# A read of PSUM ahead of the maxima, and spread factors copied by VectorE: two transformer layers on one core

## The reference

```python
for l in range(DEPTH):                      # DEPTH = 2
    h = rms_norm(x, attn_norm[l])
    proj = h @ w_in[l]
    q_lat, kv_lat, k_rope, nsa_q, nsa_kv, gate_logits = jnp.split(proj, SPLIT_POINTS, axis=-1)
    o_mla = mla_attention(...)              # 8 heads: softmax(q k^T) v, causal
    o_nsa = nsa_attention(...)              # per head: g0*o_cmp + g1*o_slc + g2*o_win
    x = x + jnp.concatenate([o_mla, o_nsa], axis=-1) @ w_out[l]
    h = rms_norm(x, ffn_norm[l])
    x = x + conv_ffn(h, ffn_w_up[l], ffn_conv_w[l], ffn_conv_b[l], ffn_w_down[l])
return rms_norm(x, final_norm)
```

## Time and profile before

| | |
|---|---|
| median of 3 runs | 1331.05 us |
| profiled execution, time | 1330.93 us |
| profiled execution, span of the core | 1329.1 us |
| granted TensorE clock, mean | 0.997 of full speed |
| TensorE busy | 1272.4 us, 96% |
| VectorE busy | 693.0 us, 52% |
| ScalarE busy | 658.0 us, 50% |
| attention steps, first layer | about 118 to 262 us |
| attention steps, second layer | about 769 to 913 us |

### The profile page before, as it was taken

The page is one execution under the profiler, slowest core; times in us unless marked ns, Lnnn a source line. Parts: engine busy times, 40 slices in busy tenths (PEclk is TensorE's granted clock), DMA queues, the critical chain, the costliest instruction groups (busy, mean ns, idle before and its releaser), DMA issues.

```text
span 1329.1 us, 18517 instructions
## 1 busy us (share of the span) xinstructions
PE 1272.4 (96%) x6626; PEld 1052.8 (79%) x6626; DVE 693.0 (52%) x1196; ACT 658.0 (50%) x1225; POOL 66.1 (5%) x153
## 2 busy tenths in 40 slices
PE   5999988999999999999999999889999999999997
PEld 4997666788888888888889867667788888888886
DVE  6435666545555555533363456673645555554334
ACT  4336788634545454323252478793444545443323
POOL 1004110001000000000000211100000000000000
PEclk9999999999999999999999999999999999999999
DMA  6320100124333333322133210012233333333211
GB/s 218 104 90 17 65 1 30 52 64 124 95 95 95 95 95 95 125 98 95 53 90 101 73 64 1 1 49 65 77 97 95 95 95 95 95 95 127 95 63 64
DMA packets 121624, 107.56 MB, mean 81 GB/s; under 512 B 3890, under 2 KB 110996, under 8 KB 121568
## 3 DMA queue, kind: packets, MB, share of 16 engines
q1 hardware_dynamic: 119344, 102.71, 25.3%
q0 software_dynamic: 1360, 3.45, 0.9%
q10 hardware_dynamic: 864, 0.66, 0.2%
HBM read 104.71 MB, written 2.10 MB: 80 GB/s over the span
## 4 chain that ended last, share of the span: by engine, by line
PE 87%; DVE 6%; ACT 3%; issue 1%; DMA 1%; SPq 0%; DVEq 0%
PE ps L1411 24%; PE ps L1412 24%; PE ps L1413 24%; PE ps L1638 4%; PE ps L1591 4%; PE ps L1572 2%; DMA raw<-in_w_in_dram 1%; PE ps L1578 1%; PE ps L1577 1%; DVE probs L1163 1%; DVE probs L1044 1%; ACT probs L842 1%; DVE x L1064 1%; DVE w_lo L575 1%; PE ps L1650 1%
## 5 line engine op out<-in xcount | busy, mean ns | idle before, releaser
L1411 PE MATMUL ps<-ht_hi,w_hi 128*128 128x512 f32 (+2 forms) x776 | 297.9, 384 | 2.5 <-DVE w_lo L575 2.5
L1412 PE MATMUL ps<-ht_lo,w_hi 128*128 128x512 f32 (+2 forms) x776 | 296.6, 382 | 0.0
L1413 PE MATMUL ps<-ht_hi,w_lo 128*128 128x512 f32 (+2 forms) x776 | 296.4, 382 | 0.0
L575 DVE TENSOR_TENSOR w_lo<-raw,w_hi 128x1024 fp32r<-128x1024 f32 (+4 forms) x196 | 218.7, 1140 | 102.3 <-ACT w_hi L568 92.7
L568 ACT ACTIVATE w_hi<-raw 128x1024 fp32r<-128x1024 f32 (+4 forms) x196 | 187.2, 982 | 100.7 <-PE ps L1413 97.1
L1327 DVE SCALAR_TENSOR_TENSOR conv<-ps,cols,conv 128x510 f32<-128x510 f32 (+1 forms) x176 | 127.6, 746 | 181.4 <-ACT conv L963 175.6
L1411 PEld LDWEIGHTS ps<-ht_hi,w_hi 128*128 128x128 f32 x776 | 146.3, 189 | 31.2 <-DVE w_lo L575 2.9
L1412 PEld LDWEIGHTS ps<-ht_lo,w_hi 128*128 128x128 f32 x776 | 146.4, 189 | 27.9 <-issue 0.5
L1413 PEld LDWEIGHTS ps<-ht_hi,w_lo 128*128 128x128 f32 x776 | 146.4, 189 | 27.7
L1411 PE MATMUL ps<-w_hi,ht_hi 128*128 128x430 f32 (+1 forms) x392 | 148.3, 378 | 4.7 <-DVE ht_lo L1051 4.0
L963 ACT ACTIVATE conv<-ps,cols 128x512 f32<-128x512 f32 x88 | 68.1, 774 | 159.9 <-PE ps L1413 159.7
(11 more groups left out here) (185 smaller groups left out, 1531.3 us busy)
## 6 DMA issues: line engine op xcount, KB each, us to landing
raw<-in_ffn_w_up_dram SPq DMA_DIRECT2D x88, 512.0 KB, 4.3
raw<-in_ffn_w_down_dram SPq DMA_DIRECT2D x44, 512.0 KB, 3.3
raw<-in_w_in_dram SPq DMA_DIRECT2D x32, 430.0 KB, 3.5
raw<-in_w_out_dram SPq DMA_DIRECT2D x16, 512.0 KB, 4.0
raw<-in_nsa_cmp_w_dram SPq DMA_DIRECT2D x8, 512.0 KB, 3.7
x<-in_x_dram SPq DMA_DIRECT2D x4, 512.0 KB, 6.2
raw<-in_mla_w_uq_dram SPq DMA_DIRECT2D x4, 384.0 KB, 3.0
out_dram<-x SPq DMA_DIRECT2D x3, 512.0 KB, 2.6
```

Of the source, the lines that this page charges most:

```text
L575: last = nc.vector.tensor_tensor(d(w_lo)[:, :, d0:d1], r(raw)[:, :, r0:r1], d(w_hi)[:, :, d0:d1].bitcast(F32), ALU.subtract)
L1411: mm(o, lhs[0], rhs[0], start=start, stop=False)
L1412: mm(o, lhs[0], rhs[1], start=False, stop=False)
L1413: return mm(o, lhs[1], rhs[0], start=False, stop=stop)
```

## The change

Three things change.

1. The addition of the compressed output to the even group's result leaves `normalize` and becomes `add_compressed(r)`, with a semaphore of its own, `cmp_read`. VectorE runs it at step 4g+8 of the odd group g, ahead of the maxima of that step. `values` of groups 6, 8 and 10 waits for `cmp_read` in place of `sum_done`.
2. ScalarE's `evac_factors` goes. VectorE copies the spread factors itself, in `normalize`, right ahead of the multiplication, and increments `fac_out` there.
3. `spread(g)` moves on TensorE from step 4g+6 to step 4g+7, ahead of `compressed` and `values`. The two tables of bank uses follow it, and the transposes get bank 5 two steps later than before.

```diff
 SCORE_USES = [(use, (0, 1, 2)) for s in range(U + LAG)
               for use in (turn_uses(s) if s < U else []) +
-              ([("f", (s - T_LAG) // T)] if s >= T_LAG and (s - T_LAG) % T == T - 1 and s < U else [])]
-TURN_USES = [(use, (3, 4) if s <= PC_STEP[1] else (3, 4, 5) if s < U else (4, 5)) for s in range(T_LAG, U + LAG)
+              ([("f", (s - LAG) // T)] if s >= LAG and (s - LAG) % T == T - 1 and s < U else [])]
+TURN_USES = [(use, (3, 4) if s <= PC_STEP[1] + 2 else (3, 4, 5) if s < U else (4, 5)) for s in range(T_LAG, U + LAG)
              for use in (turn_uses(s - T_LAG) if s < U + T_LAG else []) +
-             ([("f", NG - 1)] if s == U + T_LAG - 1 else [])]
+             ([("f", NG - 1)] if s == U + LAG - 1 else [])]
...
-                def evac_factors(g):
-
-                    act.wait_ge(fac_done, at(fac_done, l, g + 1))
-                    activate(onorm[:, g % 2, :], ps[:, FAC_BANK[g][0], :], ACT.Copy).then_inc(fac_out, 1)
...
-                    if LAG <= s < U + LAG and (s - LAG) % T == T - 1:
-                        evac_factors((s - LAG) // T)
...
+                def add_compressed(r):
+
+                    dve.wait_ge(cmp_done, at(cmp_done, l, r + 1))
+                    tt(onorm[:, 0, :], ps[:, 6, :], onorm[:, 0, :], ALU.add).then_inc(cmp_read, 1)
+
                 def normalize(g):
 
                     f = onorm[:, g % 2, :]
-                    if g >= H // 2 and g % 2 == 1:
-                        dve.wait_ge(cmp_done, at(cmp_done, l, (g - H // 2) // 2 + 1))
-                        f0 = onorm[:, 0, :]
-                        tt(f0, ps[:, 6, :], f0, ALU.add).then_inc(dve_chain, 1)
+                    dve.wait_ge(fac_done, at(fac_done, l, g + 1))
+                    v.tensor_copy(f, ps[:, FAC_BANK[g][0], :]).then_inc(fac_out, 1)
+                    dve.wait_ge(fac_out, at(fac_out, l, g + 1))
                     dve.wait_ge(pv_done, at(pv_done, l, 2 * g + 2))
-                    dve.wait_ge(fac_out, at(fac_out, l, g + 1))
                     tt(f, ps[:, out_bank(g), :], f, ALU.mult).then_inc(on_done, 1)
                     if g >= H // 2 and g % 2 == 1:
-                        dve.wait_ge(dve_chain, ch.next())
+                        dve.wait_ge(cmp_read, at(cmp_read, l, (g - H // 2) // 2 + 1))
                         dve.wait_ge(on_done, at(on_done, l, g + 1))
-                        tt(f, f, f0, ALU.add).then_inc(sum_done, 1)
+                        tt(f, f, onorm[:, 0, :], ALU.add).then_inc(sum_done, 1)
...
+                    if s > LAG + U_MLA and (s - LAG - 1 - U_MLA) % (2 * T) == 2 * T - 1:
+                        add_compressed((s - LAG - 1 - U_MLA) // (2 * T))
                     if s < U:
                         row_max(s)
...
                     elif g > H // 2 and g % 2 == 0:
-                        pe.wait_ge(sum_done, at(sum_done, l, (g - H // 2) // 2))
+                        pe.wait_ge(cmp_read, at(cmp_read, l, (g - H // 2) // 2))
...
+                    if s >= LAG and (s - LAG) % T == T - 1:
+                        spread((s - LAG) // T)
                     if s >= LAG + U_MLA and (s - LAG - U_MLA) % (2 * T) == 2 * T - 1:
                         compressed((s - LAG - U_MLA) // (2 * T))
                     if s >= LAG and s % 2 == 1:
                         values(s - LAG)
-                    if T_LAG <= s < U + T_LAG and (s - T_LAG) % T == T - 1:
-                        spread((s - T_LAG) // T)
```

More of the change, by code:

```diff
@@ L157 @@
     "sc_done": 2 * U, "max_done": 2 * U, "exp_done": 2 * U, "t_done": 6 * NG, "pt_act": U, "pt_second": U // 2,
-    "fac_ready": NG, "fac_done": NG, "fac_out": NG, "on_done": NG, "cmp_done": H // 2, "sum_done": H // 2, "pv_done": U // 2,
+    "fac_ready": NG, "fac_done": NG, "fac_out": NG, "on_done": NG, "cmp_done": H // 2, "cmp_read": H // 2, "sum_done": H // 2, "pv_done": U // 2,
     "oh_done": H, "ol_done": H,
@@ L392, in hybrid_layers @@
         cmp_done = sem("cmp_done")
+        cmp_read = sem("cmp_read")
         sum_done = sem("sum_done")
@@ L1026, in _ @@
             tt, stt = v.tensor_tensor, v.scalar_tensor_tensor
-            ch.per_layer = 2 * T + 3 + NG + H // 2 + 6 + FT
+            ch.per_layer = 2 * T + 3 + NG + 6 + FT
             dve.sem_inc(lo_done, CREDIT["lo_done"])
```

## The result

The changed kernel takes 1342.67 us (median of 4 runs, 1341.13 to 1343.58), the kernel before, run beside it, 1330.97 (1330.55 to 1331.23): ratio 1.0095, 95% interval 1.0082 to 1.0107. The change makes the kernel 0.95% slower. The profiled execution took 1343.18 us, its span is 1341.4 us, 12.3 more than before.

What follows compares the result with a forecast made beforehand. TensorE was taken to pace the attention stage, standing 11.0 us for VectorE's sum. Per layer 2.90 + 0.45 + 2 x 1.46 - 3 x 0.30 = 5.37, two layers 10.7: 1330.9 + 10.7 = 1341.6 us, range 1336 to 1348.

Steps and rivals of the forecast that it cites:

- Groups 0 to 2: First three groups of each layer: scores wait for VectorE's copy, losing 1.20, 0.87 and 0.83 us, 2.90 together.
- Odd groups: Groups 5, 7 and 9: `values` starts at 226.20 in place of 226.50, 0.30 us won each.
- Groups 3 and 4: Taken together, beside the compressed branch: most of the lateness disappears at a later turn, 0.45 us lost for both.
- Even groups 6 and 8: Scores of step 4g+9 wait for VectorE's copy, so `values` starts 1.46 us later in each.
- Group 6 is alike: The loss of 1.46 us worked out at group 8 was taken over for group 6.
- The absorption at group 4: The turn at 199.92 no longer waits 1.09 us for L938, swallowing a lateness of 1.61; if not, up to 4.7 more.
- comes back a second time: Rival: VectorE's late maxima delay exponentials and turns, TensorE pays again in 7 groups per layer: 15 us more, 1357; chance 0.07.
- only the spread, now behind it, is left: At the turn at 199.92: the turn starts where it did, and the moved spread behind it costs 0.45 us.
- the price of the gain: Rival, not slower: the copy lands before step 4g+9's scores; 13.2 us go, 1317.7; chance 0.07.
- ScalarE sets the pace: Rival: the attention stage goes at ScalarE's pace, so 24 copies of 0.60 us come back, 14.4 less, 1316.5; chance 0.04.

## Why the prediction was right, point by point

Predicted were 1341.6 us (1336 to 1348) and slower; measured 1342.67. The mechanism was the one named, and its steps were these.

- The wait of `values` for the sum is gone, and the scores of step 4g+9 wait for `fac_out` 20 times: as predicted. Predicted were about 25 us of stalls, measured 21.5. The copy takes 0.685 us (0.69 predicted), but TensorE follows 0.74 us behind its start, not 0.84: I took the 0.15 us between the sum and `values` for the semaphore's delay, and between copy and scores it is 0.05 (228.70 + 0.69 to 229.44).
- Groups 0 to 2: predicted 2.90 us, measured 2.83. Odd groups: 0.30 won, measured 0.36. Groups 3 and 4: 0.45, measured 0.28.
- Even groups 6 and 8: 1.46 each, measured 1.54 and 1.67. "Group 6 is alike" was a shortcut; its own rows give 215.34 + 0.84 + 1.09 - 215.67 = 1.60:

```profile
215.34 0.69 DVE L1190 TENSOR_TENSOR onorm<-ps,onorm 128x512 f32<-128x512 f32 x1
...
215.67 1.74 PE L1638 MATMUL ps<-probs_t,proj 128*64 128x256 f32 x16
```

- The absorption at group 4 held, at the turn that I had named: the difference of the landmarks stands at 4.47 us at step 25 and falls to 3.24 at step 27. The turn of the earlier trace rows doesn't wait for L932 in the changed kernel, and with bank 5 put back 2.8 us came back:

```profile
202.75 0.82 PE L1590 MATMUL ps<-ident,probs 128*128 128x128 f32 x6
```

- Missing from the sum, 1.4 us per layer: the later spread at step 7 (0.44) and at step 15 (0.24), a turn at step 48 that waits 0.67 for L854 (0.51), and 0.2 at group 8. There the eight transposes of the turn ahead of the scores take 1.36 us in place of 1.09, since the second four wait for ScalarE's L854, which stands behind exponentials that follow VectorE's late maxima; the maxima and the copy behind them are 0.27 late by it. That last term is the rival "comes back a second time", at a small part of its price. The other terms came out 0.3 us smaller in all, so that 6.5 stands against 5.37. I priced the spread's move at group 4 alone; its step was "only the spread, now behind it, is left", and there were such places at steps 7 and 15 as well.
- That 1341.6 lies within 1.1 us of 1342.67 is in part luck. With 0.74 in place of 0.84 the same sum gives 4.57 us per layer and 1340.0: the delay that was too long stood in for some of the missing terms. The traces' own difference is 12.3 us, the medians' 11.7.
- Clearly too large in the text was the price of the gain: "11.0 goes, and the two waits of 1.09", 1317.7. With the copy out of the way, 1323.59 was reached and with part 1 alone 1324.65, since VectorE's factors and ScalarE's evacuations were next. Only with the sum moved as well is it 1316.58.
- The rival "ScalarE sets the pace" fell: 24 copies of 0.60 us off ScalarE are worth 0.05 us, which is nothing that these runs could tell from zero, where the place is harmless. The rule of the Trainium skill weighed there (TensorEngine Tiling (Array Packing), section PSUM Bottleneck: let both engines evacuate PSUM, which the page says of matmuls made faster by tiling) decided nothing here; the place in the queue made 19 us with the engines left as they are.

## What to carry to other kernels

When a copy out of PSUM is moved to another engine, ask first which matmul gets the bank next, and what stands ahead of the copy in the new engine's queue; the load of the two engines, neither of which was the bound, made no measurable difference here. A wait that is removed shows the next chain: follow TensorE one step on, and see who must be ready there. A filler in front of a wait is free, and it costs most of its time where it is moved to.

## What the runs showed of the hardware

- A stall of TensorE can cost more than its length. Behind three of the six stalls of 2.00 us in each layer of the run with the doubled copy, and behind 1.88 + 0.42 us at one of three places in each layer of the run without part 1, the granted clock fell to 0.5, and about 1.6 us was lost each time, by the landmarks. The others of the same length had no such effect, nor had the stalls of 1.84 us before the change and those of 1.28 in the changed kernel. What tells them apart stays open.
- VectorE's copy of 128x512 fp32 out of PSUM takes 0.685 us, the same as its multiplication with an operand in PSUM, against 0.600 on ScalarE; its dependent successor starts 0.72 us behind its start, TensorE 0.74.
